# A mixture-of-experts router whose sums are taken from the unnormalised residual, with tokens on partitions

## The chip, the cores and the metric

The kernel runs on one core of a Trainium2 chip. The metric is the device time of one execution in microseconds (us); with several executions the median counts. Line numbers (L2263) are those of the kernel before. TensorE, VectorE, ScalarE and GpSimd are PE, DVE, ACT and POOL in the profile, SyncE's queue is SP. A matmul loads 128 columns of one operand into TensorE and streams the other through; the number of streamed columns is called its width here.

## What is computed

The kernel computes a conformer-like block and then a second block, on 256 tokens of 2048 features. Of the second block this matters here:

```python
h = rmsnorm_2(x, norm2_g[l]) * (1.0 + sc2[:, None]) + sh2[:, None]
x = x + g2[:, None] * moe_ffn(h, router_w, router_bias, ...)
...
aff = jax.nn.sigmoid((t @ router_w).astype(jnp.float32))     # t: 256 x 2048, router_w: 2048 x 16
score = aff + router_bias
group_score = lax.top_k(score.reshape(-1, 4, 4), 2)[0].sum(-1)
_, gsel = lax.top_k(group_score, 1)                          # one group of four experts per token
_, esel = lax.top_k(jnp.where(emask, score, NEG_INF_2), 2)   # two experts in it
w = aff[esel] / sum(aff[esel])
y = y + combine[:, e:e + 1] * ((silu(t @ w_gate[e]) * (t @ w_up[e])) @ w_down[e])
```

With residual r, scale s (the norm's gain times 1 + sc2), shift b and the root factor q of each token, t = q (r s) + b. So the router's sum is q (r · (s W)) + b · W.

## The kernel before

**Layout and tiles.** The residual lies in `pool`, features on partitions, in 16 chunks of 128x256 (`H` = 32 to 47). All large weights come as tiles of 128x2048 fp32 (1 MB) through four buffers `raw`, filled by SP's queue. Each is split in two fp32r parts: ScalarE copies the high part `w_hi` (`split`, L649), VectorE subtracts the low part `w_lo` (`lo`, L2200), both in four slots, three tiles ahead (`AHEAD`). A product is three fp32r matmuls, high by high, high by low and low by high. Activations are split the same way into `a_hi` and `a_lo`. Every engine has its own instruction stream in program order, written out by hand, with semaphores between them; there is no planner.

**The stage before.** The last 16 tiles of phase `two` are the output projection. VectorE adds each of the last four tiles into H (L2805), four chunks a tile. ScalarE then squares the chunks (L718, L725) and writes a copy scaled by s (`PRE`, L1145); GpSimd adds squares up in a lane (`lanes`, L3138).

**Router and choice** (L1894 to L1948 on TensorE, L1128 to L1170 on ScalarE, L2836 to L2925 on VectorE):
- TensorE sums the squares over partitions with a matrix of ones (`run_sums`, products 256 wide), then runs 20 products of ones by ones whose result is not used (`idle_products`).
- VectorE and ScalarE form the root and its reciprocal on 128x256 (`root`). `by_pairs` multiplies the scaled residual by it, two chunks at a time (`scaled`, L2239), and after each pair forms two low parts (`act_lo`, L2263); ScalarE adds the shift and forms the high parts (`hi_shifted`, L753).
- The router's sums are 48 products with 16 router columns loaded and 256 tokens streamed (`narrow`, L1760 to L1762), four chunks at a time. Between them TensorE turns the normalised activations to token rows (`turned_tokens`, L1906 and L1907, eight products of width 128 for each of eight groups), which ScalarE copies out (L1156); later gathers of tokens read them.
- The 16x256 sums go through ScalarE's sigmoid (L1153) and are turned (`narrow_turned`, L1768). VectorE ranks groups (L2862 to L2876), TensorE counts tokens per group (`group_counts`, L1925 to L1929, width 4), VectorE finds the order of the groups (L2879 to L2881, `group_ids`).
- SP reads the first number (L607) and loads the first expert tile in four pieces (L611), then further tiles (L623).
- VectorE then ranks experts, forms weights and three permutation matrices (L2885 to L2912), then the low part of the first expert tile in four pieces (L2921) and those of the next tiles.
- TensorE runs 10 idle products, turns the permutations (L1942, L1946), waits for all eight token copies and starts on expert 0: `first_part` (L1964 to L1966), then `big_part` (L1977 to L1979) for gate tiles 2 to 4, then four `up` tiles, with a gather behind the second.

Of the kernel before, what the change touches and what calls it, by code (L numbers as in the profile page):

```python
# [16 lines left out]
F32 = mybir.dt.float32  # L17
# [6 lines left out]
P = 128  # L24
# [333 lines left out]

def ada_place(k):

    return None if k % 4 == 3 else k - k // 4


def build(nc, tiles, ada_tiles, x_d, mem_d, params_d, crow_d, rel_rev, onehot_d, maskrow_d, ident_d,
          cmpmask_d, tab_d, sinks_d, rbias_d, router_d, gd_d, w2_d, pe_d, grp_d, tri_d, out, fbias_d):
    with ExitStack() as ctx:
# [6 lines left out]
        def sem(name):  # L373
# [48 lines left out]
                 "cmp_gelu", "cmp_tanh", "cmp_gelu_turned", "cmp_gelu_copied", "cmp_out", "cmp_ready", "cv_silu", "router_hi",  # L422
                 "router_lo", "router_sums", "router_sigmoid", "router_turned", "one_hot", "group_counts", "group_ids", "ident_r_set",
# [41 lines left out]
        KP, SQM, GSIG, RSIG = 30, 24, 62, 63  # L465
# [6 lines left out]
        GDRAW, RRAW = 60, 60  # L472
# [169 lines left out]
        def _(act):  # L642
# [96 lines left out]
            def pair_waits(name, c):  # L739

                act.wait_ge(W["normed_pairs"], 8 * FAST.index(name) + c // 2 + 1)
# [7 lines left out]
            def hi_shifted(name, src, bias):  # L749

                for c in range(DC):
# [379 lines left out]
            act.wait_ge(L["router"], 32)  # L1131
            act.wait_ge(used, BASE["moe"] - 12)
            nc.scalar.activation(hflat[:, 0:256], flat(RRAW, 1)[:, 0:256], ACT.Copy).then_inc(W["router_hi"], 1)
            for g in range(4):
# [3 lines left out]
                for c in range(4 * g, 4 * g + 4):  # L1138
# [6 lines left out]
                    nc.scalar.activation(pool[:, PRE + c, :], pool[:, H + c, :], ACT.Identity, bias=zero,  # L1145
                                         scale=scale2[:, c:c + 1]).then_inc(W["pre_ready"], 1)
# [3 lines left out]
            nc.scalar.activation(warm_root, zero, ACT.Sigmoid)  # L1150
            hi_shifted("norm2", PRE, mod[:, 48:64])
            act.wait_ge(W["router_sums"], 1)
            nc.scalar.activation(pool[0:NE, RSIG, :], psO[0:NE, 0:S], ACT.Sigmoid).then_inc(W["router_sigmoid"], 1)  # L1153
            for n in range(8):
                act.wait_ge(W["tokens_turned"], n + 1)
                nc.scalar.activation(flat(XT + 8 * (n % 2) + 2 * (n // 2), 2),  # L1156
                                     psT[:, n % 4 // 2, 512 * (n % 2):512 * (n % 2) + 512], ACT.Copy)\
                    .then_inc(W["tokens_copied"], 1)
# [161 lines left out]
        def _(pe):  # L1320
# [572 lines left out]
            run_sums("norm2")  # L1893
            idle_products(20)  # L1894
            pe.wait_ge(W["router_lo"], 1)
            pe.wait_ge(W["variance_ready"], NORM_AT["norm2"] + 1)
            pe.wait_ge(W["ident_r_set"], 1)

            def turned_tokens(n):
# [3 lines left out]
                for c in range(4):  # L1903
                    dst = psT[:, n % 4 // 2, 512 * (n % 2) + P * c:512 * (n % 2) + P * c + P]
                    ch = 4 * (n // 2) + c
                    nc.tensor.matmul(dst, a_hi[:, ch, tt * P:tt * P + P], ident_r[:, :], start=True, stop=False)  # L1906
# [3 lines left out]
            for b in range(4):  # L1910
                last = narrow(NE, "norm2", range(4 * b, 4 * b + 4))
                if b == 3:
                    last.then_inc(W["router_sums"], 1)
                else:
                    for n in range(2 * b, min(2 * b + 2, 4)):
                        turned_tokens(n)
            pe.wait_ge(W["router_sigmoid"], 1)
            narrow_turned(NE, RSIG).then_inc(W["router_turned"], 1)
# [13 lines left out]
            for n in range(4, 6):  # L1932
                turned_tokens(n)
# [4 lines left out]
            pe.wait_ge(W["perms_ready"], 1)  # L1938
            pairs = psS.rearrange("p a b -> p (a b)")
            for s in range(3):  # L1940
                for tt in range(2):
                    nc.tensor.transpose(pairs[:, s * S + tt * P:s * S + tt * P + P],  # L1942
                                        pool[:, PERM + s, tt * P:tt * P + P], ident[:, :])
            for s in range(3):
                for tt in range(2):
                    last = nc.tensor.matmul(pairs[:, 3 * S + 4 * s:3 * S + 4 * s + 4], pool[:, PERM + s, tt * P:tt * P + P],  # L1946
                                            cw[:, 4 * tt:4 * tt + 4], start=tt == 0, stop=tt == 1)
            last.then_inc(W["perms_turned"], 1)  # L1948
# [190 lines left out]
            pe.wait_ge(W["tokens_copied"], 8)  # L2139
            for stage, e in STAGES[:-1]:  # L2140
                s, j = EXPERTS[e]
                if stage == "gate":
                    for k in range(4):
                        expert_part(e, 0, k)
                        if k == 1 and e and e - 1 not in DRAINED:
# [3 lines left out]
                elif stage == "up":  # L2149
                    for k in range(4):  # L2150
# [37 lines left out]
        def _(dve):  # L2188
# [589 lines left out]

            for n, (kind, what, x) in enumerate(SECOND):
# [20 lines left out]
                if kind == "out":  # L2800
# [8 lines left out]
                    ins.then_inc(emptied["D"], 1)  # L2809
# [553 lines left out]
```

## Time and profile before

| | |
|---|---|
| median of 3 executions | 2860.99 us (2860.46 to 2868.71) |
| time of the profiled execution / its span | not marked among the three; 2868.71 is the one above the span / 2867.0 us |
| TensorE busy | 2802.2 us, 98% |
| VectorE, ScalarE, GpSimd busy | 2197.3, 1512.2, 155.9 us |
| chain that ended last | TensorE 81%, VectorE 9%, ScalarE 4%, issue 3%, DMA 2% |

Busy is the time in which an engine had an instruction in it, and matmuls overlap, so a busy TensorE is not one at its peak. The chain of waits follows the last instruction back to whatever released each step; it is the part to read for a change in a single place.

### The profile page before, as it was taken

To read this page: it belongs to the slowest core of one execution; us is meant where nothing else is said; L and a number is where in the kernel's file an instruction comes from. 1 tells how busy PE (TensorE), PEld (TensorE's weight loads), DVE (VectorE), ACT (ScalarE), POOL (GpSimd) and SP (SyncE) were. 2 spreads that over 40 slices of the span, in tenths; PEclk is the share of its full clock that TensorE was granted. 3 is DMA by queue.
4 is the path that set the end of the run, shared out by engine and by line. 5 is a ranking of instruction groups with operands and counts; after the bars stand their busy time and mean duration, and the time that the engine had idled before them with its cause. 6 is when DMAs were issued, how large, how long until landed. Compare 5 with 4: busy or idle time off the path is not lost.

```text
span 2867.0 us, 44009 instructions
## 1 busy us (share of the span) xinstructions
PE 2802.2 (98%) x17074; PEld 2487.4 (87%) x17074; DVE 2197.3 (77%) x2750; ACT 1512.2 (53%) x1731; POOL 155.9 (5%) x226
## 2 busy tenths in 40 slices
PE   8999999999999999999999999999999999999997
PEld 8888888888888789999999989999898888788886
DVE  5645458998885899999999985655765777788887
ACT  5444564444554544544444454555544555566666
POOL 3000010000101000000000020111110000000000
PEclk9999999999999999999999999999999999999999
DMA  7444444555555788888788848444415677778885
GB/s 287 176 162 176 165 166 176 187 183 188 176 212 187 282 330 325 330 329 321 308 326 320 336 163 299 175 159 164 138 64 202 258 299 269 281 305 336 341 335 220
DMA packets 116107, 692.17 MB, mean 241 GB/s; under 512 B 14288, under 2 KB 27840, under 8 KB 35328
## 3 DMA queue, kind: packets, MB, share of 16 engines
q1 hardware_dynamic: 110384, 675.33, 62.2%
q10 hardware_dynamic: 4688, 11.01, 1.2%
q0 software_dynamic: 896, 3.93, 0.4%
q8 instruction: 92, 1.51, 0.2%
q14 instruction: 47, 0.39, 0.0%
HBM read 679.74 MB, written 10.49 MB: 241 GB/s over the span
## 4 chain that ended last, share of the span: by engine, by line
PE 81%; DVE 9%; ACT 4%; issue 3%; DMA 2%; SPq 0%; DVEq 0%; ACTq 0%
PE psT L1363 12%; PE psT L1350 10%; PE psT L1337 6%; PE psT L1368 6%; PE psT L1338 6%; PE psT L1339 6%; PE psT L1351 5%; DVE w_lo L2200 5%; PE psT L1480 3%; ACT w_hi L649 2%; PE psT L1977 2%; PE psT L1978 2%; PE psT L1979 2%; DMA raw<-tiles_dram 2%; PE psT L1482 1%
## 5 line engine op out<-in xcount | busy, mean ns | idle before, releaser
L2200 DVE TENSOR_TENSOR w_lo<-raw,w_hi 128x2048 fp32r<-128x2048 f32 x531 | 1216.3, 2297 | 331.8 <-ACT w_hi L649 327.2
L649 ACT ACTIVATE w_hi<-raw 128x2048 fp32r<-128x2048 f32 x531 | 1011.5, 1910 | 368.5 <-PE psT L1339 121.3
L1363 PE MATMUL psT<-a_both,w_hi 128*128 128x512 f32 x1632 | 515.9, 398 | 6.1 <-DVE a_both L2250 2.8
L1350 PE MATMUL psT<-a_both,w_hi 128*128 128x512 f32 x1440 | 511.7, 400 | 3.5 <-issue 2.6
L1351 PE MATMUL psT<-a_both,w_lo 128*128 128x256 f32 x1440 | 404.2, 281 | 0.0
L1368 PEld LDWEIGHTS psT<-a_both,w_lo 128*128 128x128 f32 x1632 | 308.1, 189 | 72.8
L1350 PEld LDWEIGHTS psT<-a_both,w_hi 128*128 128x128 f32 x1440 | 270.5, 188 | 69.1 <-issue 4.6
L1368 PE MATMUL psT<-a_both,w_lo 128*128 128x256 f32 x1632 | 321.8, 279 | 0.0
L1351 PEld LDWEIGHTS psT<-a_both,w_lo 128*128 128x128 f32 x1440 | 272.4, 189 | 0.3
L1363 PEld LDWEIGHTS psT<-a_both,w_hi 128*128 128x128 f32 x1632 | 250.2, 190 | 7.0 <-issue 4.1
L1337 PE MATMUL psT<-a_both,w_hi 128*128 128x256 f32 x784 | 228.9, 292 | 8.7 <-DVE w_lo L2373 3.1
L1338 PE MATMUL psT<-a_both,w_hi 128*128 128x256 f32 x784 | 223.9, 286 | 0.0
L1339 PE MATMUL psT<-a_both,w_lo 128*128 128x256 f32 x784 | 223.7, 285 | 0.0
L2547 DVE CUSTOM_DVE_ANT_0 pool<-pool 128x2048 f32<-128x2048 f32 x96 | 219.4, 2285 | 4.9 <-DVE mod L2557 4.9
L1337 PE MATMUL psT<-h_hi,w_hi 128*128 128x256 f32 x752 | 216.2, 288 | 1.9 <-DVE pool L2563 1.3
L1339 PE MATMUL psT<-h_hi,w_lo 128*128 128x256 f32 x752 | 213.1, 283 | 0.0
L1338 PE MATMUL psT<-h_lo,w_hi 128*128 128x256 f32 x752 | 213.1, 283 | 0.0
L1337 PEld LDWEIGHTS psT<-a_both,w_hi 128*128 128x128 f32 x784 | 152.3, 194 | 10.0 <-DVE w_lo L2373 3.5
L967 ACT ACTIVATE pool<-pool,par 128x256 f32<-128x256 f32 x88 | 53.0, 602 | 200.6 <-DVE pool L2563 200.6
L1338 PEld LDWEIGHTS psT<-a_both,w_hi 128*128 128x128 f32 x784 | 152.5, 195 | 0.3
L1339 PEld LDWEIGHTS psT<-a_both,w_lo 128*128 128x128 f32 x784 | 152.3, 194 | 0.0
L1337 PEld LDWEIGHTS psT<-h_hi,w_hi 128*128 128x128 f32 x752 | 144.6, 192 | 4.3 <-DVE pool L2563 1.5
(443 smaller groups left out, 4927.5 us busy)
## 6 DMA issues: line engine op xcount, KB each, us to landing
raw<-tiles_dram SPq DMA_DIRECT2D x531, 1024.0 KB, 5.3
pool<-ada_tiles_dram SPq DMA_DIRECT2D x96, 1024.0 KB, 5.1
bias_rows_dram<-pool ACTq DMA_DIRECT2D x1, 8192.0 KB, 56.8
pool<-bias_rows_dram SPq DMA_DIRECT2D x40, 128.0 KB, 4.4
raw<-tiles_dram SPq DMA_DIRECT2D x12, 256.0 KB, 7.6
pool<-bias_rows_dram SPq DMA_DIRECT2D x40, 64.0 KB, 4.6
pool<-mem_dram SPq DMA_DIRECT2D x4, 512.0 KB, 8.5
pool<-x_dram ACTq DMA_DIRECT2D x1, 2048.0 KB, 11.3
```

Source lines behind the costliest of these rows:

```text
L649: nc.scalar.activation(w_hi[:, t.k % SPL, :], raw[:, t.k % RAW, :], ACT.Copy).then_inc(hi_done, 1)
L1337: nc.tensor.matmul(ps_out, wh, x_hi, start=first, stop=False)
L1338: nc.tensor.matmul(ps_out, wh, x_lo, start=False, stop=False)
L1339: return nc.tensor.matmul(ps_out, wl, x_hi, start=False, stop=last)
L1350: nc.tensor.matmul(dst.rearrange("p (h s) -> p h s", h=2), wh, a_both[:, :, a, :], start=first, stop=False)
L1351: return nc.tensor.matmul(dst[:, 0:S], wl, a_hi[:, a, :], start=False, stop=last)
L1363: nc.tensor.matmul(dst, w_hi[:, t.k % SPL, k * P:k * P + P], a_both[:, :, (k + at) % DC, :], start=k == 0, stop=False)
L1368: return nc.tensor.matmul(psT[:, t.k % 2, 0:S], w_lo[:, t.k % SPL, k * P:k * P + P], a_hi[:, (k + at) % DC, :], start=False, stop=k == DC - 1)
L1480: nc.tensor.matmul(dst.rearrange("p (h s) -> p h s", h=2), w_hi[:, slot, at:at + P], a_both[:, :, a + k, :], start=k == 0, stop=False)
L1977: nc.tensor.matmul(dst, xh, wh, start=k == 0, stop=False)
L2200: nc.vector.tensor_tensor(w_lo[:, t.k % SPL, :], raw[:, t.k % RAW, :], w_hi[:, t.k % SPL, :].bitcast(F32), ALU.subtract).then_inc(lo_done, 1)
L2547: nc.vector.tensor_tensor_reduce(out=buf, in0=buf, in1=flat(CROW, 8), scale=1.0, scalar=0.0, op0=ALU.mult, op1=ALU.add, accum_out=ada_acc[ ...
```

## The change

- `router_parts` (VectorE, behind the last but one output tile) multiplies the router's weights by s (`router_rows`, 128x256) and sums b W over the chunks of a partition (`shift_part`, 128x16).
- TensorE takes the router's sums in fp32 straight from the residual: 128 tokens of a chunk are loaded, 16 router columns are streamed (`logits`, 32 products). The squares are summed the same way into one column per 128 tokens (`column_sums`, 10 products). The 20 idle products go.
- The root factor is formed on 128x2, put on a diagonal, spread to 128x256 by one product with ones (psP) and copied by ScalarE. ScalarE's table of the sigmoid is loaded behind that copy.
- The scaled copy moves to chunks 16 to 31 (`PRE2`); its last four pairs are normalised by GpSimd, the first four by VectorE.
- VectorE scales the logits (two operations), ranks groups after four low parts and finds the order of the groups after six; the other ten low parts and the first expert tile's low part follow, then the weights, the second tile's low part and the permutations.
- TensorE turns two groups of tokens ahead of the counts and six behind them; it turns the permutations behind the second gate tile and waits for six token copies ahead of the first tile and for eight ahead of the `up` tiles. ScalarE copies tokens 7 and 8 behind the first tile's high part.

```diff
@@ ScalarE
-            act.wait_ge(L["router"], 32)
-            act.wait_ge(used, BASE["moe"] - 12)
-            nc.scalar.activation(hflat[:, 0:256], flat(RRAW, 1)[:, 0:256], ACT.Copy).then_inc(W["router_hi"], 1)
...
-            std("norm2")
+            act.wait_ge(W["variance_ready"], NORM_AT["norm2"] + 1)
+            nc.scalar.activation(rcol, router_var, ACT.Sqrt).then_inc(W["std_ready"], 1)
+            act.wait_ge(W["rstd_rows"], 1)
+            nc.scalar.activation(rstd[:, :], psP[:, 0:S], ACT.Copy).then_inc(W["rstd_copied"], 1)
             act.wait_ge(used, BASE["moe"])
+            nc.scalar.activation(warm_root, zero, ACT.Sigmoid)
             nc.scalar.activation(ident_r[:, :], ident[:, :], ACT.Copy).then_inc(W["ident_r_set"], 1)
...
+            hi_shifted("norm2", PRE2, mod[:, 48:64], range(4))
+            act.wait_ge(W["logits_scaled"], 1)
+            nc.scalar.activation(aff, aff, ACT.Sigmoid).then_inc(W["router_sigmoid"], 1)
+            hi_shifted("norm2", PRE2, mod[:, 48:64], range(4, 8))
+            token_copies(range(2))
+            hi_shifted("norm2", PRE2, mod[:, 48:64], range(8, 12))
+            token_copies(range(2, 4))
+            hi_shifted("norm2", PRE2, mod[:, 48:64], range(12, DC))
+            token_copies(range(4, 6))
...
+            token_copies(range(6, 8))
@@ TensorE
-            run_sums("norm2")
-            idle_products(20)
+            pe.wait_ge(W["router_ready"], 1)
+            nc.tensor.matmul(psR, ones[:, :], shift_part, start=True, stop=True).then_inc(W["router_sums"], 1)
+            logits(range(2))
+            pe.wait_ge(W["lanes_added"], 3 * RUN.index("norm2") + 3)
+            column_sums(LANE, True, False)
+            for c in range(4):
+                pe.wait_ge(W["last_squares"], 4 * RUN.index("norm2") + c + 1)
+                last = column_sums(SQ + 4 + c, False, c == 3)
+                if c < 3:
+                    logits([2 + c])
+            last.then_inc(W["sums_part"], 3)
+            logits(range(5, 8))
+            pe.wait_ge(W["rstd_ready"], ROOT_AT["norm2"] + 1)
+            nc.tensor.matmul(psP[:, 0:S], ones[:, :], flat(RDIAG, 1), start=True, stop=True).then_inc(W["rstd_rows"], 1)
+            logits(range(8, DC)).then_inc(W["router_sums"], 1)
...
-            for b in range(4):
-                last = narrow(NE, "norm2", range(4 * b, 4 * b + 4))
...
+            for n in range(2):
+                turned_tokens(n)
...
             group_counts()
-            for n in range(6, 8):
+            for n in range(2, 8):
                 turned_tokens(n)
             idle_products(10)
...
-            pe.wait_ge(W["tokens_copied"], 8)
+            pe.wait_ge(W["tokens_copied"], 6)
...
                         expert_part(e, 0, k)
+                        if k == 1 and e == 0:
+                            turned_perms()
@@ VectorE
+                if n == len(SECOND) - 2:
+                    router_parts()
...
-            root("norm2", D)
-            by_pairs("norm2", PRE, rstd[:, :], bias=mod[:, 48:64])
+            nc.vector.tensor_scalar(router_var, psC, 1.0 / D, EPS, ALU.mult, ALU.add).then_inc(W["variance_ready"], 1)
+            dve.wait_ge(W["std_ready"], NORM_AT["norm2"])
+            link(nc.vector.reciprocal(rcol, rcol))
+            nc.vector.tensor_tensor(flat(RDIAG, 1)..., ident..., rcol..., ALU.mult).then_inc(W["rstd_ready"], 1)
+            dve.wait_ge(W["rstd_copied"], 1)
+            pair_scaled(0)
+            pair_scaled(1)
+            pair_lo(0)
+            pair_scaled(2)
+            pair_lo(1)
+            dve.wait_ge(W["router_sums"], 2)
+            for tt in range(2):
+                ins = nc.vector.scalar_tensor_tensor(aff[:, NE * tt:NE * tt + NE], psL[:, NE * tt:NE * tt + NE],
+                                                     rcol[:, tt:tt + 1], shift_row, ALU.mult, ALU.add)
+            ins.then_inc(W["logits_scaled"], 1)
+            pair_scaled(3)
...
+            pair_lo(2)
             dve.wait_ge(W["group_counts"], 1)
...
+            for p in range(3, 8):
+                pair_lo(p)
+            first_tile()
...
+            lo(Tile(BASE["moe"] + 1))
@@ GpSimd, behind lanes("norm2", SQ, LANE)
+            pl.wait_ge(W["rstd_copied"], 1)
+            pl.wait_ge(W["pre_ready"], 32)
+            for p in range(POOLED, 8):
+                pair = chunks(PRE2 + 2 * p, 2)
+                nc.gpsimd.tensor_tensor(pair, pair, rstd[:, :].unsqueeze(1).to_broadcast([P, 2, S]), ALU.mult)\
+                    .then_inc(W["pairs_pooled"], 1)
```

## Rows read from the trace of the kernel before

**Rows 1.** The page of the kernel before: its head

```profile
span 2867.0 us, 44009 instructions
```

**Rows 2.** Chain of waits, 2138 to 2181 us: start us, us, what

```profile
2140.33 0.49 DVE pool L2805
...
2144.51 0.43 DVE var L2217
...
2147.20 1.29 DVE pool L2239 x2
...
2159.55 0.31 PE psY L1768 x2
...
2164.04 0.25 DVE idx_big L2881 x2
...
2167.39 7.37 DMA raw<-tiles_dram
2174.84 1.93 ACT w_hi L649
2176.79 2.30 DVE w_lo L2200
2179.14 0.50 PE psT L1977
```

**Rows 3.** TensorE's timeline around the router: start us, us, instructions, idle before

```profile
2151.17 0.23 PE L1906 MATMUL psT<-ident_r,a_both 128*128 128x128 f32 x1
...
2152.79 0.28 PE L1907 MATMUL psT<-ident_r,a_both 128*128 128x128 f32 x1
...
2158.81 0.28 PE L1762 MATMUL psY<-a_both,h_lo 128*16 128x256 f32 x1
...
2162.24 0.39 PE L1925 MATMUL psY<-small,ones 128*128 128x4 f32 x2 [0.21 <-DVE small L2873]
...
2163.38 0.42 PE L1906 MATMUL psT<-ident_r,a_both 128*128 128x128 f32 x1
...
2166.80 4.10 PE L1324 MATMUL psY<-ones 128*128 128x128 f32 x20
2170.74 0.82 PE L1942 MATMUL psY<-ident,pool 128*128 128x128 f32 x6
2171.39 1.40 PE L1946 MATMUL psY<-small,pool 128*128 128x4 f32 x12
2172.65 0.48 PE L1964 MATMUL psT<-w_hi,a_both 128*128 128x512 f32 x1
...
2177.99 0.39 PE L1966 MATMUL psT<-w_hi,a_both 128*128 128x512 f32 x1
```

**Rows 4.** Stretches: length, busy us per engine, then TensorE clock, DMA share, GB/s

```profile
2020.00:2022.00 2.00, 0.45 (x2) 0.02 (x1) 0.00 (x0) 1.51 (x3) 0.00 (x0) 1.00 0.88 233
2022.00:2024.00 2.00, 1.34 (x5) 1.21 (x6) 0.00 (x0) 2.00 (x2) 0.00 (x0) 0.87 0.98 383
...
2163.00:2164.00 1.00, 1.00 (x8) 1.00 (x8) 0.33 (x2) 0.00 (x0) 0.00 (x0) 0.71 0.00 0
2170.00:2172.00 2.00, 2.00 (x20) 2.00 (x19) 1.12 (x3) 1.26 (x2) 0.00 (x0) 0.94 0.97 340
```

**Rows 5.** Groups by shape, 2140.3 to 2179.2 us: count | busy us, mean ns | idle before

```profile
L2263 DVE SCALAR_TENSOR_TENSOR a_both<-pool,mod,a_both 128x256 fp32r<-128x256 f32 x16 | 6.9, 482 | 0.0
L2239 DVE TENSOR_TENSOR pool<-pool,rstd 128x512 f32<-128x512 f32 x8 | 5.4, 688 | 0.0
...
L1150 ACT ACT_TABLE_LOAD x1 | 1.3, 1283 | 0.0
```

**Rows 6.** Timelines of GpSimd and of VectorE near 48 us

```profile
48.04 1.36 POOL L3128 TENSOR_TENSOR pool<-pool 128x512 f32<-128x512 f32 x1 [12.04 <-ACT pool L718]
49.48 2.67 POOL L3130 TENSOR_TENSOR pool<-pool 128x256 f32<-128x256 f32 x1
...
48.28 3.27 DVE L2200 TENSOR_TENSOR w_lo<-raw,w_hi 128x2048 fp32r<-128x2048 f32 x1
```

More of the change, by code:

```diff
@@ L1153, in _, with token_copies @@
[L1153 to L1158, printed above, removed]
+            def token_copies(part):
+                for n in part:
+                    act.wait_ge(W["tokens_turned"], n + 1)
+                    nc.scalar.activation(flat(XT + 8 * (n % 2) + 2 * (n // 2), 2),
+                                         psT[:, n % 4 // 2, 512 * (n % 2):512 * (n % 2) + 512], ACT.Copy)\
+                        .then_inc(W["tokens_copied"], 1)
@@ L1892, in _, with logits, column_sums @@
                         mix_sums(m)
-            run_sums("norm2")
-            idle_products(20)
-            pe.wait_ge(W["router_lo"], 1)
-            pe.wait_ge(W["variance_ready"], NORM_AT["norm2"] + 1)
+            def logits(part):
+                for c in part:
+                    if c < 12:
+                        pe.wait_ge(emptied["D"], OWN[:BASE["moe"] - 3 + c // 4].count("D"))
+                    elif c < 15:
+                        pe.wait_ge(W["tail_chunk"], 3 + c - 11)
+                    else:
+                        pe.wait_ge(emptied["D"], OWN[:BASE["moe"]].count("D"))
+                    for tt in range(2):
+                        last = nc.tensor.matmul(psL[:, NE * tt:NE * tt + NE], pool[:, H + c, tt * P:tt * P + P],
+                                                router_rows[:, NE * c:NE * c + NE], start=c == 0 and tt == 0, stop=c == DC - 1 and tt == 1)
+                return last
+            def column_sums(src, first, end):
+                for tt in range(2):
+                    last = nc.tensor.matmul(psC[:, tt:tt + 1], pool[:, src, tt * P:tt * P + P], ones[:, 0:1],
+                                            start=first and tt == 0, stop=end and tt == 1)
+                return last
+            pe.wait_ge(W["router_ready"], 1)
+            pe.wait_ge(W["variance_ready"], NORM_AT["norm2"])
+            nc.tensor.matmul(psR, ones[:, :], shift_part, start=True, stop=True).then_inc(W["router_sums"], 1)
[12 more added lines that the diff above has]
+            logits(range(8, DC)).then_inc(W["router_sums"], 1)
             pe.wait_ge(W["ident_r_set"], 1)
@@ L1930, in group_counts, with turned_perms @@
                     .then_inc(W["group_counts"], 1)
-            for n in range(4, 6):
-                turned_tokens(n)
             group_counts()
-            for n in range(6, 8):
+            for n in range(2, 8):
                 turned_tokens(n)
             idle_products(10)
[L1938 to L1948, printed above, removed]
+            def turned_perms():
+                pe.wait_ge(W["perms_ready"], 1)
+                pairs = psS.rearrange("p a b -> p (a b)")
+                for s in range(3):
+                    for tt in range(2):
+                        nc.tensor.transpose(pairs[:, s * S + tt * P:s * S + tt * P + P],
+                                            pool[:, PERM + s, tt * P:tt * P + P], ident[:, :])
+                for s in range(3):
+                    for tt in range(2):
+                        last = nc.tensor.matmul(pairs[:, 3 * S + 4 * s:3 * S + 4 * s + 4],
+                                                pool[:, PERM + s, tt * P:tt * P + P],
+                                                cw[:, 4 * tt:4 * tt + 4], start=tt == 0, stop=tt == 1)
+                last.then_inc(W["perms_turned"], 1)
             def weights(t, at, n):
```

89 lines of the change are left out of this document (55 added, 34 removed).

## The prediction

> **What bounds the kernel now.** The page, read first, shows TensorE as the engine that nearly fills the span of 2867.0 us [rows 1]. An edit off its path gains nothing, and this change touches one of the few places where it waits. The chain of waits, read second, shows that place. The last sums of the output projection are emptied from 2140.33; the sum of squares is ready at 2144.51, the first pairs are normalised at 2147.20, the affinities are turned at 2159.55, the group numbers are found at 2164.04 to 2164.29, the DMA of the first chosen expert's second weight tile runs from 2167.39 to 2174.84, its high part takes 1.93 us on ScalarE, its low part 2.30 us on VectorE, and TensorE starts on it at 2179.14 [rows 2]. From there the chain is matmuls. So 38.8 us pass between dense stretches, and 14.9 of them follow from the choice by a fixed train (load, two splits). TensorE's own timeline, third, tells what it does meanwhile: router products, 64 turning products, idle products from 2166.80, permutations from 2170.74, the first expert tile from 2172.65 [rows 3]. The granted clock, fourth, has the two levels 1.0 (2.4 GHz) and 0.5 (1.2 GHz). A mean of 0.71 over 2163 to 2164 is 0.58 us at the lower one, so it fell at 2163.4; 0.94 over 2170 to 2172 puts its return at 2170.2; 0.87 over 2022 to 2024 is a fall near 2023.5 [rows 4]. So 6.8 us of the gap ran at 1.2 GHz. The change must be judged by when TensorE starts the third gate tile, because it moves the permutations behind the second. Before: 2179.14 plus one tile. A tile is 24 products, 2172.65 to about 2178.2, 5.5 us [rows 3]. That gives **2184.65**.
>
> **The sum, step by step.** Small VectorE and ScalarE work of some 0.2 us each is taken at that.
>
> *Weights of the router, shift sums.* Three VectorE operations of at most 256 columns, in a slack after the last but one output tile; one operation of 256 columns leaves ScalarE there. Nothing, as VectorE waits for TensorE there; without that cover about 1 us.
>
> *Router sums.* Removed are 48 products of 256 columns and the two turnings; added are 32 fp32 products with 16 columns, one for the shift, 10 column sums and one of 256 columns. The nearest row is the 128x4 product: 12 records, 2 for a product, start 0.105 apart (2171.39 to 2172.65); five such products from 2162.24 to 2163.38 give 0.114 [rows 3]. I take 0.23 for a product. The Trainium skill (TensorE: Matmul & The Clock Gate, Wait — 56ns, not 53.3ns?) gives a floor of about 25 ns between matmul starts however narrow; by it the 32 products would cost 1.6 us instead of 7.4. The trace disagrees: each record here brings new weights, and none is under 0.1.
> Until the last column sum TensorE has 21 such products in its queue behind the last tile: 4.8 us, so 2145.2 against 2144.51 now.
>
> *The clock.* This decides. TensorE now keeps full rate here with 20 idle fp32 products and 256-column sums; the change takes both away, and from 2140.33 to the turnings nearly all its products have 1 or 16 columns. In the profile it fell at 2163.4 although TensorE counted as busy for 1.00 of that microsecond; before it came 4-column products from 2162.24, and the last 256-column one had begun at 2158.81. Near 2023.5 it fell behind an engine busy for 0.45 of 2020 to 2022, after a tile that so ended about 2020.4 [rows 3, 4]. At the same distances from 2140.33 it falls between 2143.4 and 2145; I take 2144.5. It stayed low through the turnings of 2163.38 to 2166.80 and came back while the idle products ran [rows 3, 4]. At 1.2 GHz 16 turnings take 3.42 us (2163.38 to 2166.80) against 1.74 (2151.17 to 2152.79 and one more); 20 idle records take 3.9 [rows 3]. For a narrow product at 1.2 GHz no row exists: from 0.23 (unchanged) to 0.43 (the same factor 1.9). I take 0.42, because the nearest row, the turnings, is bound by loading weights as these are, and doubled.
>
> *To the scaled logits.* Variance, root, reciprocal and diagonal: four small operations and their hand-overs, 1.2 us from 2145.5 (the last column sum is already at the lower clock). TensorE must first finish logits 5 to 7 (6 x 0.42): 2148.0; the rows' product of 256 columns takes 0.85 at this clock; ScalarE copies 0.42: 2149.4, 2.2 us later than the 2147.20 of before. The 16 products of chunks 8 to 15 queue behind it: 6.7 us, 2155.6. Meanwhile the table load of 1.28 us [rows 5], until now hidden under the 256-column reciprocal, stands ahead of ScalarE's first high part. VectorE and GpSimd share the pairs. Near 48 us their tensor-tensor work shut each other out: VectorE's split took 3.27 instead of 2.30 behind a GpSimd instruction begun 0.24 earlier, and GpSimd's next 128x256 took 2.67 [rows 2, 6]. So GpSimd's four pairs (1.3 each, 1.36 by rows 6) delay VectorE by up to 5.4 us, where four on VectorE cost 4 x 0.69 [rows 5]; here most fall into its waits. I charge one, 1.3.
>
> *To the choice.* Logits 2155.6, scaled 0.3, sigmoid and fourth pair 1.5, ranking 2.1 (of the 2.4 between the turned affinities and the counts, rows 2, 3): one-hot at 2159.6. Counts 5 x 0.42: 2161.8; numbers 0.7: 2162.6, **1.7 us earlier** than 2164.29. At full rate it would be 5.9 (rival 1); that is what the edit moves out of the way, 16 low parts of 0.43 [rows 5] and two turnings, less the new steps. Pieces and tiles land 1.7 earlier: the second at 2173.1.
>
> *To the experts.* VectorE's other 10 low parts (4.3 us) and its first split now stand ahead of the weights' ranking; TensorE's turnings 2 to 7 stand behind the counts. Six groups of 8 at 0.214 are 10.3, with 0.5 of waits: 2172.6. Ten idle products, 3.9, give 2176.2 [rows 3], where the clock is back. First tile until 2181.7. The second was split at about 2179.0, so nobody waits: 2187.2. The permutations, now here, take 1.9 (2170.74 to 2172.65, rows 3): third tile at **2189.1**.
> Against 2184.65 that is **4.5 us later**. Behind the permutations' wait ScalarE holds the fourth tile's high part: 0.95 + 1.9 + 2.3 = 5.2 against a tile of 5.5, so covered by 0.3; with that cover gone each further tenth is on the path. SP's queue loses nothing: its piece loads wait for the numbers alone, and tile 5's for the first split, which is ahead of it. Everything later is the same work.
>
> **The rivals.**
> 1. *The clock holds.* The same steps at full rate: logits end at 2150.4 and are scaled by 2152.6, behind VectorE's first low parts; numbers are there at 2158.4 (5.9 earlier), turnings end at 2164.5, ten idle products take 2.3, the first tile starts at 2166.8, the second at 2173.5 behind its low part (VectorE's queue now sets it), the third at 2181.0: **3.6 us faster**, 5.2 if GpSimd delays nobody. For it: TensorE's instruction stream has few holes. The Trainium skill (same page, What's actually happening) has the gate follow how busy the engine was; on the word busy alone this rival would be right. Against: the 1.00 busy microsecond in which it fell [rows 4]. Chance 0.22.
> 2. *The clock comes back late, in the first expert tile.* Mechanism: turnings at 1.2 GHz did not lift it, and now six groups of them precede the idle products. Price: a 5.5 us tile at the factor 1.9 is 5 us more, 9.5 in all: **slower**, decided by whether the granted clock reads 0.5 in the first tile. Chance 0.1.
> 3. *The choice is earlier, or not, and it does not matter.* If narrow products keep 0.23 at the lower clock, logits and counts end some 3 us earlier, and the turnings, which still take 10.3, end so too, unless ScalarE's last high parts hold them: 2 us slower than before. If the choice is not earlier at all, the second tile's low part still has 2.7 us in hand (2179.0 against 2181.7), and the forecast stands. Chance of its own 0.1.
> The forecast has the remaining 0.58.
>
> **How the numbers follow.** The profiled execution spans 2867.0; of the three times 2868.71 alone is above this, so I take it as its own, 7.7 above the median 2860.99. The sum makes it 2873.2, and for the median 2860.99 + 4.5 = **2865.5**. The forecast's own range is +1 to +7 (fall of the clock 1 us earlier or later, narrow products at either price): 2862 to 2868. Rival 1 reaches 2855.8, rival 2 2870.5. With both ends: 2856 to 2870.5. About 0.3%, 8.6 us, is what a measurement can tell from no change. The forecast, rivals 1 and 3 lie within it, so same 0.86; slower is rival 2 with about 0.1; faster would need more than even rival 1 gives, 0.04.
>
> **What would show it.** Right: granted clock 0.5 soon after 2144 and until the idle products; records of the 16-column products 0.2 apart behind that; group numbers only 1 to 3 us earlier, counted from the last tile's end; permutations between the second and third gate tile, 1.9 us, with no wait; VectorE's tensor-tensor work held up by GpSimd once or twice. Wrong: clock at 1.00 until the turnings (rival 1), a tile of 10 us (rival 2), TensorE waiting for a low part of the third or fourth tile, or a difference that arises before 2140 or in later experts.

## The result and the profile after

The changed kernel takes 2869.04 us (median of 20, 2861.97 to 2876.95) against 2862.76 for the kernel before in the same comparison (median of 20, 2858.39 to 2868.74): the ratio is **1.0021, 95% interval 1.0012 to 1.0029**, which is 6.0 us slower (3.4 to 8.3). The forecast was 4.5 us slower, inside the 0.3% that a measurement can hardly tell.

Two executions of the kernel before differ by several microseconds at other places, where short stretches at the lower clock come and go. So all places are told as a distance, T+, from the first emptying of the last output tile (2140.33 before, 2141.84 after), with starts taken from the timelines. "Third tile" is the start of the third gate tile: 2184.75 or T+44.4 before, 2192.30 or T+50.5 after. The difference is **6.0 us**, as much as the two kernels differ in time. The two profiled spans alone don't show this: they differ by 1.1, because the rest behind the third tile is 6.5 us shorter in the changed kernel's profile (682.3 and 675.8). A second profile of each has 676.3 and 676.7 there, so that 6.5 is scatter between executions. That the loss arises at this one place rests on the two distances, 6.0 and (second profiles) 7.2.

The page's head and the chain of waits of the changed kernel (start us, us, what; the chain counts a matmul from the end of the one before, so it starts up to 0.3 later than in the timeline):

```profile
span 2868.1 us, 43994 instructions
...
2150.72 1.05 PE psY L1950 x2
2151.79 0.39 ACT rstd L1158
2152.21 2.36 DVE pool L2921 x2
2154.57 2.82 DVE a_both L2319 x2
2157.39 1.67 DVE pool L2921
...
2162.79 0.59 PE psY L1974 x2
...
2165.52 0.25 DVE idx_big L2991 x2
...
2166.00 0.49 DVE a_both L2319
2166.54 0.48 PE psT L1962
...
2176.19 3.43 PE psY L1346 x20
2179.62 0.23 PE psT L2016
...
2192.44 0.34 PE psT L2029
```

Against [rows 2] the load and the two splits are gone from the chain. From the first row to the last TensorE is the bound, but for the copy of the root factor, a stretch on VectorE (2152 to 2163, with the ranking of groups at its end) and the numbers at 2165. The group numbers come at 2165.76, T+23.9, where they were at T+24.0: the choice is not earlier at all. TensorE's timeline of the changed kernel shows why:

```profile
2141.78 1.04 PE L1925 MATMUL psY<-pool 128*128 128x16 f32 x8
2142.67 1.03 PE L1932 MATMUL psY<-ones,pool 128*128 128x1 f32 x8
...
2147.14 0.99 PE L1932 MATMUL psY<-ones,pool 128*128 128x1 f32 x4
...
2151.55 6.85 PE L1925 MATMUL psY<-pool 128*128 128x16 f32 x32
2158.24 0.45 PE L1962 MATMUL psT<-ident_r,a_both 128*128 128x128 f32 x1
...
2164.94 0.45 PE L1962 MATMUL psT<-ident_r,a_both 128*128 128x128 f32 x1
...
2175.99 3.63 PE L1346 MATMUL psY<-ones 128*128 128x128 f32 x20
2179.38 0.47 PE L2016 MATMUL psT<-w_hi,a_both 128*128 128x512 f32 x1
```

Four narrow products (8 records) take 0.89 us at first, 0.22 each; 16 (32 records) take 6.7 later, 0.42 each. The router's 256-wide products of before are gone, but TensorE has hardly a gap left up to the first tile (0.19, 0.45 and 0.50 us). Stretches of the changed kernel (length, busy us per engine, then TensorE clock, DMA share, GB/s):

```profile
2142.00:2144.00 2.00, 2.00 (x20) 2.00 (x20) 1.58 (x5) 1.65 (x5) 0.00 (x0) 1.00 0.00 0
2144.00:2146.00 2.00, 2.00 (x13) 2.00 (x12) 0.00 (x0) 1.66 (x5) 0.00 (x0) 0.58 0.01 4
...
2160.00:2162.00 2.00, 2.00 (x11) 2.00 (x11) 1.83 (x12) 1.82 (x6) 0.00 (x0) 0.50 0.00 0
2176.00:2178.00 2.00, 2.00 (x10) 2.00 (x10) 1.83 (x14) 1.77 (x2) 0.00 (x0) 0.50 0.97 397
2178.00:2180.00 2.00, 2.00 (x16) 1.92 (x15) 1.73 (x11) 1.40 (x2) 0.00 (x0) 0.89 1.07 442
```

A mean of 0.58 over two microseconds is 0.32 us at full level, so the clock fell at 2144.3 (T+2.5), with TensorE counted busy for 2.00 of 2.00 us before and after; 0.89 puts its return at 2178.4. That is **34.1 us at 1.2 GHz in one stretch, where it was 6.8** [rows 4]. VectorE's and GpSimd's timelines of the changed kernel, behind one row of the kernel before:

```profile
2148.47 0.88 DVE L2263 SCALAR_TENSOR_TENSOR a_both<-pool,mod,a_both 128x256 fp32r<-128x256 f32 x2
...
2152.21 2.36 DVE L2921 TENSOR_TENSOR pool<-pool,rstd 128x512 f32<-128x512 f32 x2 [2.98 <-ACT rstd L1158]
2154.50 2.90 DVE L2319 SCALAR_TENSOR_TENSOR a_both<-pool,mod,a_both 128x256 fp32r<-128x256 f32 x2
2157.32 1.75 DVE L2921 TENSOR_TENSOR pool<-pool,rstd 128x512 f32<-128x512 f32 x1
...
2152.25 6.27 POOL L3314 TENSOR_TENSOR pool<-pool,rstd 128x512 f32<-128x512 f32 x4 [10.42 <-ACT rstd L1158]
```

In the kernel before, where GpSimd does nothing here, these three groups take 1.29, 0.88 and 0.69 us [rows 2, 5]; beside GpSimd's four pairs they take 2.36, 2.90 and 1.75, **4.15 us more**. When GpSimd ends, at 2158.5, VectorE is quick again. The logits end at 2158.4 and are scaled only at 2159.78. How the two engines shut each other out is called the lock below.

### The profile page after: what moved, and what is told of

Read it like the earlier page. It is cut to its first block, busy times and chain, and to the rows that moved or that the text cites. A ratio compares the mean times of both kernels' runs of the same rounds, so it can differ in the third digit from the quotient of the medians.

```text
span 2868.1 us, 43994 instructions
## 1 busy us (share of the span) xinstructions
PE 2810.4 (98%) x17062; PEld 2499.5 (87%) x17062; DVE 2197.4 (77%) x2751; ACT 1510.3 (53%) x1731; POOL 162.1 (6%) x230
## 4 chain that ended last, share of the span: by engine, by line
PE 85%; DVE 9%; ACT 3%; issue 2%; DMA 0%; SPq 0%; DVEq 0%; ACTq 0%
PE psT L1385 12%; PE psT L1372 10%; PE psT L1359 6%; PE psT L1390 6%; PE psT L1361 6%; PE psT L1360 6%; PE psT L1373 5%; DVE w_lo L2256 4%; PE psT L1502 3%; PE psT L2029 2%; PE psT L2031 2%; PE psT L2030 2%; ACT w_hi L657 2%; PE psT L2040 1%; PE psT L2042 1%
```

## The experiments

The theory to be tested: TensorE's long stretch at the lower clock, which comes from the narrow products, is the loss, and its bound is TensorE's own instruction stream. Rivals: the lock between GpSimd and VectorE; the order of work in the tail (permutations, idle products, the second tile's low part). All distances are T+ in us, from one profile each; numbers is when VectorE has the order of the groups; at half is the time at 1.2 GHz around the router. Times are ratios to the kernel before with their 95% intervals; single executions scatter too widely to stand there.

| kernel | numbers | first tile | third tile | at half, us | time |
|---|---|---|---|---|---|
| before | 24.0 | 32.3 | 44.4 | 6.8 | |
| before, again | 24.8 | 33.9 | 44.9 | 10.2 | |
| change | 23.9 | 37.5 | 50.5 | 34.1 | 1.0021 (1.0012 to 1.0029) |
| change, again | 24.3 | 38.7 | 52.1 | 37.5 | |
| before, no 20 idle products | 26.8 | 35.1 | 47.2 | 17.1 | |
| before, late permutations | 23.9 | 30.3 | 47.7 | 10.2 | |
| before, GpSimd pairs | 32.8 | 41.7 | 53.1 | 20.5 | |
| change, VectorE pairs | 22.8 | 37.6 | 50.5 | 34.1 | |
| change, no late idle products | 21.8 | 32.0 | 46.6 | 30.7 | |
| change, wide products | 21.4 | 35.9 | 48.8 | 20.5 | 1.0024 (1.0015 to 1.0033) |
| wide, fillers | 19.3 | 36.0 | 49.0 | 13.7 | 1.0014 (1.0001 to 1.0027) |
| narrow, fillers | 24.5 | 43.3 | 56.2 | 20.5 | 1.0030 (1.0014 to 1.0047) |
| wide, short tail | 19.1 | 28.6 | 43.6 | 13.7 | 0.9997 (0.9988 to 1.0007) |
| narrow, short tail | 22.7 | 32.2 | 47.2 | 34.1 | 1.0000 (0.9990 to 1.0010) |

**The same kernels again.** No edit.

> The changed kernel, unaltered, a second profile of it. In one profile the clock fell 2.5 us behind the last output tile and stayed at half for 34.1 us, and the form without the late products, which is the same up to there, had it fall 5 us behind it and its numbers 2.1 us earlier. If the point where it falls moves from execution to execution: a fall at 2 to 6 us, numbers at 21.5 to 24, third gate tile at 48 to 50.5, and 31 to 34 us at the half clock. If the point is fixed by the code: 2.5, 23.9 and 50.5 again, and the earlier numbers come from the late products' absence.

> The kernel before, unaltered, a second profile of it: how far its own third gate tile (44.3 us) moves. If the clock's fall moves by a few microseconds from execution to execution, 6.8 us at half at the turnings may become 3.4 or 10.2, and the distance 43 to 46; if not, 44.3 again. Either way its stretch at half stays under a third of the changed kernel's.

In the changed kernel the clock fell at T+2.1 this time (granted 1.00 over 2140 to 2142, 0.50 over 2142 to 2144) and stayed low for 37.5 us; the third tile came at 52.1, 1.6 beyond the expected range. Before: 44.9, with 10.2 us at half. So one profile's distance is good to some 1.6 us, and the two pairs differ by 6.0 and 7.2 us.

**The kernel before without its 20 idle products.**

```diff
             run_sums("norm2")
-            idle_products(20)
```

> The kernel before without its 20 idle products behind the squares' sums. Measured by the distance from VectorE's first emptying of the last output tile to TensorE's first product of the third gate tile: 44.3 us in the kernel before (2140.33 to 2184.65), 50.6 in the changed one (2141.84 to 2192.44). Clock theory (the loss of the change is the 1.2 GHz clock, 34.1 us of it in place of 6.8, because its products around the router are 1 and 16 columns wide and the idle ones are gone): TensorE then does nothing from about 4 us to 9 us behind the last output tile, the clock falls in the router's first products, comes back under its 256-column products, and the distance grows by 1 to 5 us, to 45 to 49. Rival theories (GpSimd locks VectorE out; the new order of the work behind the choice): the idle products are on nobody's path, 44.3 +- 0.5.

Numbers and third tile come 2.8 us later than in the first profile of the kernel before (2.0 and 2.3 later than in the second); the clock falls at T+6.3 instead of T+23, while TensorE waits, and the first router products run at half. The idle products that the change takes away had been worth 2 to 3 us.

**GpSimd's pairs alone, in the kernel before.**

```diff
-                    if p < 7:
+                    if p < (3 if name == "norm2" else 7):
                         scaled(p + 1)
@@ GpSimd, behind lanes("norm2", SQ, LANE)
...
+            for p in range(4, 8):
...
+                nc.gpsimd.tensor_tensor(pair, pair, rstd...to_broadcast([P, 2, S]), ALU.mult).then_inc(W["pairs_pooled"], 1)
```

> The kernel before with one part of the change alone: GpSimd multiplies the last four normalised pairs, VectorE the first four. Theory (while GpSimd works on pairs, VectorE's own pair operations stretch from 1.3 to 2.4 us and from 0.9 to 2.9 us, some 4 us in all in the changed kernel): VectorE saves four products of 0.69 us and loses 4, so the groups' numbers come 0 to 2 us later (24 to 26 us against 23.95), third gate tile at 44.3 to 46.3. Rival (the offload is a gain, the loss in the changed kernel comes from the narrow products alone): numbers up to 2.4 us earlier, third gate tile at 42 to 43.5.

VectorE's timeline of this kernel:

```profile
2141.04 2.38 DVE L2242 TENSOR_TENSOR pool<-pool,rstd 128x512 f32<-128x512 f32 x2
2143.33 2.90 DVE L2266 SCALAR_TENSOR_TENSOR a_both<-pool,mod,a_both 128x256 fp32r<-128x256 f32 x2
2146.15 1.75 DVE L2242 TENSOR_TENSOR pool<-pool,rstd 128x512 f32<-128x512 f32 x1
```

The lock costs the same as in the changed kernel, within 0.02 us a row. The numbers are not 0 to 2 but **8.9 us later**. The low part for which TensorE waits is done at T+14.2 instead of T+10.0, which is the lock's 4.1. Meanwhile TensorE was busy for only 0.77, 0.50 and 0.59 us of three stretches of 2 us, the clock fell at T+12.4, and the router products and turnings that follow ran at half; the other 4.7 us arise there. The offload is no gain; both theories had missed what the wait does to the clock.

**VectorE's pairs in the changed kernel** (`POOLED = 8`).

```diff
-POOLED = 4
+POOLED = 8
@@ VectorE
             pair_lo(2)
+            pair_scaled(4)
+            pair_scaled(5)
             dve.wait_ge(W["group_counts"], 1)
...
+            pair_scaled(6)
+            pair_scaled(7)
```

> The changed kernel with all eight pairs normalised by VectorE, the last four where it waits for the counts and behind the group numbers; GpSimd does none. Clock theory: the logits end at 2158.4 whatever GpSimd does, and VectorE scaled them at 2159.8, so at most 1.4 us come back ahead of the choice; distance 49 to 50.6, granted clock as before (about 34 us at 0.5). Lock theory: GpSimd's four instructions held VectorE back by 4.1 us (2.36, 2.90 and 1.75 for what takes 1.29, 0.86 and 0.69), and those come back: 46 to 47.

VectorE's and TensorE's timelines of this kernel, behind the numbers:

```profile
2168.13 1.29 DVE L2921 TENSOR_TENSOR pool<-pool,rstd 128x512 f32<-128x512 f32 x2
2169.34 2.46 DVE L2319 SCALAR_TENSOR_TENSOR a_both<-pool,mod,a_both 128x256 fp32r<-128x256 f32 x6
...
2169.88 0.47 PE L1962 MATMUL psT<-ident_r,a_both 128*128 128x128 f32 x1 [1.71 <-DVE a_both L2319]
```

With the clock falling at the same T+2.5, the numbers come 1.1 us earlier and the third tile at 50.5 as in the change, as the clock theory had it. But the rows show where the 1.1 went: the last two pairs, 1.29 us, now stand ahead of the next low part on VectorE, and TensorE waits 1.71 us for it instead of 0.50. So this form doesn't show that the lock costs nothing; a form in which TensorE doesn't wait there is measured below (narrow, short tail).

**Late permutations, in the kernel before.** The first tile's low part ahead of the ranking, the second's ahead of the permutation matrices, permutations behind the second gate tile, as in the change.

```diff
+                        if k == 1 and e == 0:
+                            turned_perms()
@@ VectorE
+            lo(Tile(BASE["moe"] + 1))
```

> The kernel before with only the order behind the choice changed as in the change: the first expert tile's low part ahead of the ranking of experts, the second's ahead of the permutation matrices, the permutations turned behind the second gate tile. The router's sums stay as they were. By the steps of the prediction: the second gate tile stays bound by its load (2179.14), the permutations' 1.9 us move from under that load onto the path: distance 46.2 (+1.9). Order theory (the order is the whole loss): 50. A theory in which the order gains, as it starts the first tile's split earlier: 43 to 44.

The first tile starts 2.0 earlier, but the second waits 2.58 us for its low part and starts at T+38.6, where it did before (38.8). A 3.4 us stretch at half follows in it, then the permutations of 1.9 us: third tile 3.3 later, 1.5 beyond the expected 46.2. The move gives back more than it brings when the choice itself isn't earlier.

**Wide products in the changed kernel.** Router columns loaded and 256 tokens streamed, squares and root on 128x256 as before, affinities turned.

```diff
-                    for tt in range(2):
-                        last = nc.tensor.matmul(psL[:, NE * tt:NE * tt + NE], pool[:, H + c, tt * P:tt * P + P],
-                                                router_rows[:, NE * c:NE * c + NE], ...)
+                    last = nc.tensor.matmul(psL, router_rows[:, NE * c:NE * c + NE], pool[:, H + c, :], start=c == 0, stop=c == DC - 1)
```

> The changed kernel with the router's fp32 sums turned round: 16 router columns loaded, 256 tokens streamed (16 products 256 columns wide in place of 32 of 16 columns), squares summed 256 wide with a matrix of ones and the root formed on 128x256 as in the kernel before, affinities turned behind the sigmoid. Same sums from the unnormalised residual, same order behind the choice, GpSimd keeps its four pairs, no idle products between. Clock theory: granted clock 1.0 up to the turnings at least; the group numbers come 15 to 18 us behind the last output tile's emptying in place of 23.9, and the distance is 38 to 44, so the time 0 to 6 us under the kernel before. Lock theory: numbers at 20 or later and the distance over 46. If the clock falls in the six groups of turnings, up to 5 us more than the low end.

The clock now held to T+15.5, and fell in the turnings. Stretches of this kernel:

```profile
2148.00:2150.00 2.00, 0.12 (x2) 0.16 (x2) 2.00 (x3) 0.51 (x1) 1.98 (x2) 1.00 0.00 0
2150.00:2152.00 2.00, 1.75 (x11) 1.49 (x11) 2.00 (x5) 0.95 (x3) 0.00 (x0) 0.82 0.00 0
```

The logits were done at T+10.9 instead of 16.6, but VectorE, held by GpSimd, scaled them at T+13.0, and TensorE stood idle for 3.2 us. The numbers came at 21.4, not at the 15 to 18 of the clock theory, and the third tile at 48.8, 1.6 us earlier than in the change and not at 38 to 44: both are what the lock theory had said (20 or later, over 46). The time (1.0024) is no better. Direction alone doesn't mend it.

**Fillers.** Products of ones between the narrow products and the turnings and ahead of the column sums (narrow), or behind the logits and between the turnings, with all pairs on VectorE and 4 instead of 10 idle products behind the last turnings (wide).

```diff
@@ narrow, fillers
                 for c in part:
+                    idle_products(2, psP[:, S:S + P] if c < 8 else psS[:, 0, 0:P])
@@ turned_tokens, in both
+                idle_products(2)
@@ wide, fillers
             logits(range(3, DC)).then_inc(W["router_sums"], 1)
+            idle_products(12)
```

> The change, with products of ones by ones (128 columns, results unused) put between the narrow ones on TensorE: two ahead of each chunk's logit products, one ahead of each pair of column sums, two ahead of each group of turnings. Nothing is taken out and nothing moved. Distances are from the first emptying of the last output tile to the first gate product of the third expert tile (44.3 us in the kernel before, 50.5 in the changed one). Clock theory (it is the half clock, 34.1 us of it in the changed kernel, that makes the narrow products, the counts and the turnings dear, and it falls because nothing wide runs): if the added products hold the clock, the narrow product takes 0.23 us instead of 0.43, a group of turnings 0.9 instead of 1.7; the added ones cost some 0.06 us each at full clock, 61 of them 3 to 4 us, mostly in place of waits; third gate tile at 42 to 47 us, and the stretch at the half clock is under 20 us. Rival (the distance is set by VectorE's and GpSimd's pair work, whatever TensorE's clock does): the clock rises or not, and the third tile stays at 50 to 53. If the clock does not hold in spite of the added products, each costs 0.11 us and the distance becomes 52 to 56, and the clock theory is not tested.

> The form with the router's columns loaded and 256 tokens streamed (as in the kernel before, with sums of squares and root as there, affinities turned afterwards), all eight normalised pairs on VectorE in pieces, 12 products of ones behind the logits, two ahead of each group of turnings, and 4 instead of 10 behind the last. Clock theory: the clock stays at full level from the last output tile to the first expert tile or falls only for 3.4 us; turnings 0.9 us a group; numbers at 19 to 21 us, first tile at 29 to 33 (before 32.3), third gate tile at 42 to 45 (before 44.3, the same form without fillers 48.8). Then the time is 0 to 2 us under the kernel before. Rival (fillers do not hold the clock against narrow loads): numbers as before or later than 21.4, third gate tile at 49 to 52.

TensorE's timeline with narrow products and fillers:

```profile
2152.73 0.69 PE L1346 MATMUL psY<-ones 128*128 128x128 f32 x4
2153.26 0.52 PE L1926 MATMUL psY<-pool 128*128 128x16 f32 x4
2153.63 0.69 PE L1346 MATMUL psY<-ones 128*128 128x128 f32 x4
...
2160.15 1.20 PE L1346 MATMUL psY<-ones 128*128 128x128 f32 x4
```

The fillers do hold the clock: it fell at T+22.9, where it fell between T+2.1 and T+4.8 in five profiles with narrow products and no fillers, and two narrow products take 0.37 us where they took 0.85. But two fillers take 0.53, not the 0.12 that I had reckoned, so a chunk costs 0.90, more than the 0.85 at half clock without them, and the third tile comes at 56.2 instead of 42 to 47. The wide form was expected at 42 to 45 and 0 to 2 us under the kernel before; it came at 49.0 and at 1.0014. In both kernels the clock fell all the same (T+22.9 in the counts, T+22.4 in the turnings), where two fillers then cost 0.8 a group. So in these kernels what TensorE runs decides whether the clock holds behind the last output tile. It also refutes the way out.

**Without the ten late idle products** (`idle_products(10)` behind the last turnings goes).

> The change without the ten products of ones behind the last turnings. In the changed kernel they take 3.4 us at the half clock ahead of the first expert tile, at 37.5 us. Theory (the first tile is ready by then, so they are in the way; but the second tile's low part is what comes next): first tile at 34.1 us, begun at the half clock, so 2.7 us longer; second tile at 40 to 43.1; third gate tile at 48 to 50.5. Rival (the first tile's weights are not ready earlier either): nothing moves, the time is idle instead of busy. Below 48 would mean that these products alone account for more than a third of the loss.

TensorE's timeline at the end of its turnings:

```profile
2169.24 0.41 PE L1963 MATMUL psT<-ident_r,a_both 128*128 128x128 f32 x1
2169.46 0.73 PE L2016 MATMUL psT<-w_hi,a_both 128*128 128x512 f32 x1
2169.99 0.63 PE L2017 MATMUL psT<-w_lo,a_both 128*128 128x512 f32 x1
...
2173.71 0.40 PE L2018 MATMUL psT<-w_hi,a_both 128*128 128x512 f32 x1
```

The first tile starts 5.5 earlier than in the change, at half clock until about 2173, and takes 7.2 instead of 5.6 us; the third tile is 3.9 earlier. 2.1 of that is luck: this execution's clock fell at T+4.8, and its numbers came at 21.8. What remains, 1.7, is the 3.4 us of idle products less the 1.7 of a slower tile.

**The short tail.** All pairs on VectorE, two moves ahead of the counts, no late idle products; once with wide products and ten fillers behind the logits, once with narrow ones and none.

```diff
             pair_lo(2)
+            pair_scaled(4)
+            pair_lo(3)
             dve.wait_ge(W["group_counts"], 1)
...
-            idle_products(10)
```

> The form with the router's columns loaded and 256 tokens streamed, all normalised pairs on VectorE (scaled 4 and low part 3 ahead of the wait for the counts), 10 products of ones behind the logits, none between the turnings and none behind them. In the form with 12, two a group and 4, the turnings ended 34 us behind the last output tile, 9 us of that in the added products (0.25 us each at full clock, 0.41 at half), and the groups' numbers were there at 19.3. Theory (with the numbers early, TensorE's own turnings are what the first tile waits for): without them the turnings end at 26 to 28 us, the first tile starts at 29 to 32 (its load of 7 to 8 us behind the numbers now being the bound), third gate tile at 41 to 44.3; the clock falls in the turnings all the same, at 16 to 22 us. Time 0 to 3 us under the kernel before. Rival (the second tile's cast and low part, queued on ScalarE and VectorE behind token copies, low parts and the second ranking, hold the third tile whatever the turnings do): first tile early, second at 39 or later, third at 45 to 47.

> The changed kernel with its narrow products as they are, but with the pairs and the tail of the form that is level with the kernel before (all normalised pairs on VectorE, scaled 4 and low part 3 ahead of the wait for the counts, nothing behind the last turnings): against that form only the direction of the router's products differs (and the 10 products of ones behind its logits). Theory (the narrow products are the larger part of the loss, by the half clock they leave behind): clock at half from 2 to 5 us behind the last output tile on, numbers at 21 to 23.5 (19.1 in the other form), turnings end at 31 to 33, third gate tile at 45.5 to 48 (43.55 in the other form, 50.5 and 52.1 in the changed kernel), time 2 to 4 us above the kernel before. Rival (GpSimd's pairs and the late products are the whole loss): third gate tile at 43 to 45, time within 1 us of the kernel before.

Stretches of the wide form:

```profile
2158.00:2160.00 2.00, 1.53 (x13) 1.29 (x12) 1.91 (x8) 0.91 (x2) 0.00 (x0) 1.00 0.00 0
2160.00:2162.00 2.00, 1.17 (x8) 0.98 (x7) 1.95 (x4) 1.06 (x3) 0.00 (x0) 0.57 0.02 4
```

With the clock up until T+19.4 the numbers come at T+19.1, 4.9 us before those of the kernel before, and the third tile at 43.6. The time is level with before. Narrow products in the same order give 47.2, so in distance the direction (with the ten fillers) is worth 3.7 us; but the time is level with before too (interval 2.9 us either way), not 2 to 4 us above it as I had expected.

Against the change, the narrow form's turnings end at T+32.2 instead of T+34.2, with the clock falling at T+2.6 and no wait of TensorE in them. So the pairs on GpSimd had cost some 1.9 us of distance after all (one profile each). The 3.4 us of idle products go too, and the first tile, at half, takes 7.6 instead of 5.6: together the 3.2 by which its third tile is earlier.

What this says of the theory: in distance it holds in part. In time it isn't shown. The narrow form with the short tail keeps the whole 34.1 us at half and is level with the kernel before, while the change with wide products has 20.5 at half and is as slow as the change. The measured loss went with the tail (GpSimd's pairs and the late idle products; the wide form also gained its ten fillers) in both pairs of kernels, 1.0021 to 1.0000 and 1.0024 to 0.9997, and with the direction in neither. Since the narrow form's third tile is still 2.8 us later than before, and its time is known to 2.9 only, how the 6.0 us divide between direction and tail stays open. No form beat the kernel before by more than can be measured.

## Why the prediction was right

- *Number.* 4.5 us slower forecast, 6.0 (3.4 to 8.3) measured, inside the forecast's own +1 to +7. The median of 2869.04 is above the 2862 to 2868 that went with it, 1.8 of that because the kernel before has a median of 2862.76 over 20 executions, not 2860.99. Some luck is in the agreement: the moment at which the clock falls alone moves the numbers by 2 us between executions, and two errors of 1.3 and 1.4 us were partly made good by one of 1.0 the other way (below).
- *Place and sign.* Right: 6.0 against 4.5 between the last output tile and the third gate tile. The forecast laid it on the clock: at full rate (rival 1) its steps gave 3.6 faster. The experiments bear this out for a part of the distance and not for the time.
- *Clock.* Predicted to fall at T+4.2 and return in the idle products; it fell at T+2.5 (2.1 to 4.8 in other executions of the same products) and returned at 2178.4, in the idle products, just ahead of the first tile. Rival 2 was near: in the second profile of the change the clock returned 0.9 us into that tile, and without the idle products the tile ran its first 3.6 to 4.5 us at half. Rival 1, the clock holds, fell, and with it the reading of the Trainium skill (TensorE: Matmul & The Clock Gate, What's actually happening) by the word busy alone: here TensorE is busy 2.00 of 2.00 at a granted 0.50.
- *Narrow product.* 0.23 and 0.42 predicted, 0.22 and 0.42 measured. The price taken from the nearest row by its kind was good. (Its factor of 1.9 is 1.97 by its own rows, 3.42 over 1.74.)
- *Column sums, root, copy.* Predicted to put the first normalised pair at T+9.1, measured T+10.4; with the early fall of the clock the sums ended 1.4 later.
- *GpSimd's lock.* VectorE's operations were stretched by 4.15 us, nearer to the upper bound of 5.4 than to the 1.3 charged. What reached the path was as charged: the logits ended at T+16.6 and were scaled at T+17.9, 1.4 later, and all pairs on VectorE brought the numbers forward by 1.1. The 1.3 stands in no line of the sum by itself, though, so the sum had no wait for VectorE there. The Trainium skill (SBUF — State Buffer, SBUF: two separate sides) says that one of the two holds the shared ports for its whole instruction while the other is blocked. The rows agree with this in part: alone GpSimd's four pairs would take some 5.2 us (estimate, 4 times the 1.29 of L3128 in the kernel before) and VectorE's five operations 2.9, in turn 8.0 with nothing shared; side by side they took 6.9 (2152.21 to 2159.07).
- *Choice.* 1.7 us earlier predicted (T+22.3), 0.0 measured (T+23.9). The logits ended 1.3 later than in the sum (T+16.6 against T+15.3), VectorE came to them 1.4 later still, and scaling, sigmoid, fourth pair and ranking took 3.0 instead of 3.9. This step is the one that was off, and it is the whole difference between forecast and distance. The sign of 1 to 3 us earlier numbers did not come.
- *Tail.* From the numbers: turnings 10.0 predicted, 10.2 measured; idle products 3.6 and 3.4 (the prediction names 3.9, but adds 3.6); two tiles and permutations 12.9 and 12.9. The second tile's low part was not waited for, as said. Half right was rival 3, that the choice does not matter: it was not earlier, and the rest of the forecast stood. Where it was 1.1 earlier (VectorE's pairs) the third tile did not move, but because of a new wait for VectorE, not of ScalarE's high parts, which rival 3 had named.

## What to carry to other kernels

Replacing wide products by narrow ones with new weights each removes streamed columns, not time: here a 256-wide product took 0.12 us from start to start, and a 16-wide one, in two records, 0.22. It can also take the clock away from what follows, even though the busy share rises to 100%: price the stretch behind it at the lower level. Look at the granted clock, not the busy time, before idle products go, and count what each costs where it stands (0.23 to 0.26 us here at full clock). Sharing elementwise pairs between GpSimd and VectorE cost more than it saved in both orders tried: some 1 to 2 us in the change, and 8.9 us with a wait of TensorE behind it. And a place in one profile is not the time: two forms whose third tiles lay 3.7 us apart could not be told apart in time.

## What was not expected of the hardware

- In all four forms that came to the counts and turnings at full level the clock fell there (T+15.5, 19.4, 22.4, 22.9). In each TensorE had waited shortly before (3.2, 0.5, 2.5 and 1.1 us), so the turnings alone are not shown to be the cause. At half, six groups of turnings with no gap over 0.5 us did not raise it; it came back in the idle products or 0.9 to 4.5 us into the 128x512 products of the first tile.
- The same code dropped the clock at T+2.1, 2.5 or 4.8 in different executions, which moves the numbers by 2 us.
- The lock's cost repeated within 0.02 us a row in two kernels.
